# Two blocks on one core: other order at the opening, router, first gather and out-projection, and another form of the last norm

## The chip, the cores and the metric

The kernel runs on one core of a Trainium2 chip. The metric is device time in microseconds (us), lower is better. The engines are named as in the profile: PE multiplies matrices, PEld loads the weights it multiplies by, DVE, ACT and POOL compute elementwise, and SP only issues transfers. ACTq and SPq are the queues on which ACT and SP issue their DMAs; an engine that issues a DMA does nothing else meanwhile. Products are accumulated in PSUM, in eight banks of 128 x 512 floats.

## The reference

512 tokens of width 1024 pass two different blocks. All is fp32.

```python
# first block
h = layer_norm(x, ln_in_g, ln_in_b)
mix = token_mixer(h, ...)              # projections, causal conv, gated delta rule, gating, out-projection
h = layer_norm(ALPHA * h + mix, ...)
ffn = hier_moe(h, ...)                 # router (4 groups x 8), top 2 of 32 experts
h = layer_norm(ALPHA * h + ffn, ln2_g, ln2_b)
# second block, on 16 meta tokens + 512 tokens
xn = rmsnorm(h, norm1_g)
q, k, v, xr, gr, g_merge = split(xn @ w_in)
a = softmax(rope(q) @ rope(k).T) @ v
xc = centred_dwconv(xr, conv_w, conv_b)
r = rg_lru(xc, ..., lam, forward) and (..., reverse)     # uses log_sigmoid(lam)
h = h + merge(a, r, gr, g_merge) @ w_out
h = h + ffn(rmsnorm(h, norm2_g))       # rmsnorm: y = x * rsqrt(mean(x*x) + eps) * g
```

## The kernel before, in words

Every product is made exact to fp32 by splitting both operands into a high part (rounded to fp32r, a form that PE multiplies fast) and a low part (the rest), and by three matmuls per product: low x high, high x high, high x low. The high part of a weight or activation is mostly made by ACT or DVE (a copy), the low part by DVE or POOL (a subtraction of high from raw). Names: `W` raw weights, `WHU`/`WL` high and low of a piece of `w_in`, `HT` turned activations, `HTH`/`HTL` their parts.

Each engine runs a program written out by hand (`s_...` on ACT, `v_...` on DVE, `g_...` on POOL, `p_...` on PE, `q_...` on SP), and engines wait for each other by semaphores. The weights come through a ring of 2 MB slots on SP's queue, load `n` by `q_weight(n)`; `w_room` adds waits to some of them.

The program passes these stages:

- **Opening.** `x` is normed, turned by PE (eight tiles T0 to T7) and split, and the first pieces d0, d1, d2 of `w_in` are split. ACT issues seven loads on its own queue (`L499`, `L500`, `L823` to `L826`) before its first split. POOL also casts a table of constants `lv` (`L517`, used only by the delta rule).
- **Delta rule, merge, first out-projection, norm.**
- **Router.** PE makes the logits tile by tile; DVE adds, finds groups and top 2, ranks tokens and writes the token list `toki`. DVE's cast `oneb` stands ahead of the first logits' evacuation (`L253 ST<-ps,ST`). POOL clears the table `BG[0:64, 8:16]`, from which the gathered rows of expert inputs are read in full (64 rows, two buffers per ring entry).
- **First gather.** POOL gathers 64 rows (0.26 MB) of `h1d` per expert by indirect DMA, each landing in a ring of four. ACT's queue, after PE's last logits, loads rows of `ln2_g`, `ln2_b`, the meta tokens and the rope table; SP's queue loads the weights for slot 6 (2 MB, tile `HT`) at the same time.
- **32 experts**, loop over `b` with PE, DVE and ACT in lockstep, weights streaming.
- **Combine, norm, second block's projections and rope.** `s_lambda` and `v_lambda` make log_sigmoid(lam) for the RG-LRU; they stand at the start of `s_middle`, `v_middle`.
- **Attention**, woven on PE with the convolved columns of `xr` and further projections. `scores(i)` makes the scores of 128 queries into a pair of banks; ACT and DVE make the softmax; `turned(i)` turns the probabilities (form `cst,M`). `pairs` is the list of free pairs of banks. The projection of an x granule of `xr` (kind `"x"`) also takes a pair, which comes free when DVE has read it for the convolution (`L256`, then `L259` x3).
- **RG-LRU**, then **second out-projection**: eight tiles `("out", m, y)`, one per bank, each summed over eight inputs (`VL`, `WO` parts of the merged rows; `WOH`, `WL` parts of `w_out`). The last RG-LRU products (`s6`, `s7`) lie in banks 1 and 0.
- **Last norm**: H is added up by DVE (`v_added`), squared by ACT (`s_squared`), scaled by the inverse rms by ACT (`s_normed3`), turned by PE (`p_turn3`), multiplied by the gain and moved out of PSUM by DVE (`v_gain3`, into `HT`), split high by ACT (`s_turn3`, `XH`) and low by DVE (`v_low3`, `XL`). **FFN** follows, its weight parts in `WS`.

Of the kernel before, what the change touches and what calls it, by code (L numbers as in the profile page):

```python
# [167 lines left out]
def build(nc, a, cst_d, rope_d, out):  # L168
    ctx = ExitStack()
    with ctx:  # L170
# [291 lines left out]
        def q_load():  # L462
            for i in range(NT):
                q.e.dma_start(H[:, i, :], a["x"][0, i * P:(i + 1) * P, :]).then_inc(c_x[i], 16)
                if i == 0:
                    q.e.dma_start(cst[:, :], cst_d[:, 0:C_LV]).then_inc(c_cst, 16)
            for n in range(2):
                q_weight(n)

        def q_zero(part):  # L470

            q.wait_ge(first_done, 2)
# [19 lines left out]
        def s_load():  # L492
# [81 lines left out]
        JOBS = [("d", 0)] + [("T", k) for k in range(8)] + [("d", 1), ("d", 2), "ab"] + [("d", n) for n in range(3, 24)]  # L574
# [108 lines left out]
        def s_evac(n):  # L683
            t, x = B["d", n], xps[n % 3]
            s.wait_ge(*t.full())
            if n < 3:
                s.wait_ge(first_done, 2)
            else:
                s.wait_ge(conv_done, n - 2)
# [415 lines left out]
        def v_head(h):  # L1105
# [6 lines left out]
            v.wait_ge(first_done, 1)  # L1112
# [112 lines left out]
        def g_head(h):  # L1225
# [15 lines left out]
            for n in range(1, 7):  # L1241
                if n == 1:
                    g.wait_ge(first_done, 1)
# [452 lines left out]
        rt_in, rt_out, ms_done, dst_done = sem("router_in"), sem("router_exp"), sem("counts"), sem("rows")  # L1696
# [58 lines left out]
        def s_router():  # L1755
            s.wait_ge(rt_in, 1)
# [4 lines left out]
        def g_router():  # L1761
# [3 lines left out]
            g.e.memset(BG[0:BLK, 8:16, :], 0.0).then_inc(g.up())  # L1765
# [96 lines left out]
        def v_rows():  # L1862
# [6 lines left out]
            v.wait_ge(rt_out, 1)  # L1869
            v.e.tensor_reduce(pgs, gx, AX.X, ADD).then_inc(v.up())  # L1870
            v.wait_ge(rt_out, 2)
# [183 lines left out]
        def s_experts():  # L2055
            s.wait_ge(*B["lg", 3].full())
# [4 lines left out]
            s_expert_x(0)  # L2061
            for b in range(NE):
# [31 lines left out]
        def v_experts():  # L2094
            for b in range(NE):
# [5 lines left out]
                if b == 1:  # L2101
                    v_over_rows()
                if b == NE - 2:
# [18 lines left out]
        def g_experts():  # L2122
# [3 lines left out]
            g.wait_ge(*g.now)  # L2126
# [353 lines left out]
        class Front:  # L2480


            def __init__(self):
# [3 lines left out]
                self.due = []  # L2487

# [138 lines left out]
        def p_second(f, singles, pairs):  # L2627
            for j, (kind, n) in GRAN3:
                o = gr_buf(j)
                p.wait_ge(*gr_low(j))  # L2630
                if kind == "x":
# [9 lines left out]
                    pairs.append(b)  # L2641
                    gr_read[j] = t.full()
# [506 lines left out]
        def v_middle():  # L3149
            f = Front()  # L3150
            ts(v, qg, pcol(QNG), 128.0 ** -0.5, None, MUL, None).then_inc(qg_done)
            v_lambda()
# [8 lines left out]
        def s_middle():  # L3161
            f = Front()
            s_lambda()
# [23 lines left out]
        n2_rms, n2_inv, n2_done = sem("n2_rms"), sem("n2_inverse"), sem("n2_normed")  # L3187
        x3_hi, x3_lo = sem("x3_high"), sem("x3_low")
# [48 lines left out]
        def v_rms3(m):  # L3237
            v.wait_ge(n2_rms, m + 1)
            v.e.reciprocal(ssr[:, m:m + 1], ssr[:, m:m + 1]).then_inc(n2_inv)

        def v_out():
# [6 lines left out]
            v_gain3(0)  # L3248
            v_added(3)
            v_rms3(2)  # L3250
            v_low3(0)
            v_gain3(1)
            v_rms3(3)
            v_low3(1)
            v_gain3(2)
            v_gain3(3)
            v_low3(2)
            v_low3(3)
# [4 lines left out]
        def v_gain3(i):  # L3263
            for h in range(2):
                t = B["x3", i, h]
                v.wait_ge(*t.full())
                tt(v, x3_at(HT, i, h), four(t.at),
                   pc[:, N2G + 4 * h:N2G + 4 * h + 4].unsqueeze(2).to_broadcast([P, 4, P]), MUL).then_inc(t.drained)

        def v_low3(i):  # L3270
            z = slice(i * P, (i + 1) * P)
            v.wait_ge(x3_hi, 2 * i + 2)
            tt(v, XL[:, :, z], HT[:, 0:8, z], XH[:, :, z].bitcast(F32), SUB).then_inc(x3_lo)
# [8 lines left out]
        def s_out():  # L3282
# [5 lines left out]
            s_normed3(0)  # L3288
            s_squared(2)
            s_normed3(1)  # L3290
            s_turn3(0)
            s_squared(3)
            s_normed3(2)
            s_normed3(3)
            s_turn3(1)
            s_turn3(2)
            s_turn3(3)

        def s_normed3(m):
            s.wait_ge(n2_inv, m + 1)  # L3300
            act(XN[:, m, :], H[:, m, :], ACT.Copy, scale=ssr[:, m:m + 1]).then_inc(n2_done)

        def s_turn3(i):
# [283 lines left out]
```

## Time and profile before

| | us |
|---|---|
| median of 3 runs | 2288.48 (2287.21 to 2293.30) |
| profiled execution | 2291.81 |
| its span in the trace | 2290.0 |

| stretch of the span, us | PE busy | DVE busy | PEclk | GB/s |
|---|---|---|---|---|
| 0 to 31.5, opening | 5.89 | 13.91 | 0.83 | 284 |
| 834 to 860.3, router and first gather | 6.77 | 22.49 | 0.50 | 377 |
| 860.3 to 1369, experts | 429.79 | 63.43 | 0.91 | 387 |
| 1530 to 1727, attention | 169.24 | 102.68 | 0.97 | 54 |
| 1860.4 to 1919.7, out-projection and last norm | 50.82 | 38.59 | 0.90 | 87 |
| 1919.7 to 2290, FFN | 363.89 | 111.56 | 0.99 | 83 |

PE is busy for 2064.2 of 2290.0 us (90%). PEclk is the clock that PE was granted, as a share of the full one. In the table a row with PE busy for nearly all of its length is at PE's rate; one where PE is idle has another limit, which the timeline names in brackets.

### The profile page before, as it was taken

The numbers are of one execution on the slowest core, as the hardware profiler recorded it, in microseconds if no ns is written. First come the engines' busy times: TensorE is split into PE (matmuls) and PEld (weight loads), VectorE is DVE, ScalarE is ACT, GpSimd is POOL, SyncE is SP. The second block draws the span as 40 slices with busy tenths as digits, with TensorE's granted clock in tenths as the row PEclk, the third lists the DMA queues.
The fourth block names the chain that finished last, engine by engine and source line by source line (L and its number), as shares of the span: only waits on it lengthen the run. The fifth ranks groups of instructions, "written<-read, shape, count | busy, mean of one in ns | idle before, by whom it ended". The sixth has DMA issues, their size and how long they took to land.

```text
span 2290.0 us, 24322 instructions
## 1 busy us (share of the span) xinstructions
PE 2064.2 (90%) x10160; PEld 1515.5 (66%) x10160; DVE 950.8 (42%) x1370; ACT 644.4 (28%) x969; POOL 454.5 (20%) x311
## 2 busy tenths in 40 slices
PE   5999999999999969888788879898898888999999
PEld 4879888888887753333333337676665666888787
DVE  6864444433323661111011125864554883222333
ACT  3442332321323201000000024343135754222221
POOL 4432132232332511111111011320002310000021
PEclk8899999999999979999899989999999998999999
DMA  4662231221324367999999964302111033322220
GB/s 156 202 184 61 56 88 42 38 74 38 74 37 150 138 246 306 407 410 410 403 412 412 417 280 173 108 2 82 46 47 46 37 111 110 110 94 90 84 82 37
DMA packets 97513, 360.75 MB, mean 158 GB/s; under 512 B 9834, under 2 KB 34572, under 8 KB 85112
## 3 DMA queue, kind: packets, MB, share of 16 engines
q1 hardware_dynamic: 84752, 332.76, 40.4%
q0 software_dynamic: 8240, 19.00, 2.5%
q10 hardware_dynamic: 4408, 7.40, 1.0%
q8 instruction: 82, 1.34, 0.2%
q14 instruction: 31, 0.25, 0.0%
HBM read 338.41 MB, written 29.10 MB: 160 GB/s over the span
## 4 chain that ended last, share of the span: by engine, by line
PE 79%; DVE 9%; ACT 5%; issue 5%; POOL 1%; DMA 1%; ACTq 0%; SPq 0%; DVEq 0%; POOLq 0%
PE ps L269 75%; PE ps L273 4%; ACT ST L265 1%; DVE H L259 1%; ACT L265 1%; DVE ST L253 1%; DVE BG L253 1%; ACT M L265 1%; DVE WL L253 0%; POOL WL L253 0%; DVE ST L2829 0%; DMA BG<-h1d,toki 0%; DVE BG L259 0%; DVE ML L253 0%; ACT M L266 0%
## 5 line engine op out<-in xcount | busy, mean ns | idle before, releaser
L269 PE MATMUL ps<-W,BG 128*64 128x512 f32 x672 | 202.1, 643 | 31.5 <-issue 31.4
L269 PE MATMUL ps<-XH,WS 128*128 128x512 f32 x704 | 218.6, 392 | 0.0
L269 PE MATMUL ps<-HTH,WL 128*128 128x512 f32 x448 | 182.4, 407 | 0.0
L269 PEld LDWEIGHTS ps<-ST 128*128 128x128 f32 x1376 | 168.4, 193 | 8.7 <-POOL ST L253 1.7
L269 PE MATMUL ps<-ST 128*128 128x64 f32 (+1 forms) x1376 | 168.7, 274 | 1.2 <-POOL ST L253 1.0
L269 PEld LDWEIGHTS ps<-XH,WS 128*128 128x128 f32 x704 | 133.5, 190 | 28.0
L269 PE MATMUL ps<-M,BG 128*64 128x512 f32 (+1 forms) x336 | 122.1, 550 | 31.2 <-DVE H L259 13.7
L2100 DVE COPY BG<-ps 128x512 f32<-128x512 f32 x32 | 22.1, 692 | 302.0 <-PE ps L269 302.0
L269 PE MATMUL ps<-XL,WS 128*128 128x512 f32 x352 | 138.3, 393 | 5.0 <-DVE XL L253 5.0
L269 PEld LDWEIGHTS ps<-W,BG 128*64 128x64 f32 x672 | 61.6, 147 | 120.8 <-issue 119.5
L263 ACT ACTIVATE BG<-ps 128x512 f32<-128x512 f32 x48 | 28.5, 595 | 381.3 <-PE ps L273 350.0
L269 PE MATMUL ps<-X2H,GV 128*128 128x512 f32 (+1 forms) x512 | 129.6, 344 | 0.0
L269 PE MATMUL ps<-ST,BG 128*64 128x512 f32 (+2 forms) x304 | 106.1, 566 | 11.7 <-issue 10.9
L269 PE MATMUL ps<-WS,HH 128*128 128x512 f32 x352 | 109.7, 393 | 2.6 <-issue 2.6
L269 PEld LDWEIGHTS ps<-HTH,WL 128*128 128x128 f32 x448 | 88.5, 198 | 20.5
L253 POOL TENSOR_TENSOR WS<-W,WS 128x1024 fp32r<-128x1024 f32 x11 | 26.3, 2392 | 379.8 <-ACT WS L263 379.8
L263 ACT ACTIVATE ST<-ps 128x256 f32<-128x256 f32 (+3 forms) x128 | 44.3, 353 | 196.0 <-PE ps L269 117.2
L269 PEld LDWEIGHTS ps<-X2H,GV 128*128 128x128 f32 x512 | 89.5, 192 | 13.5 <-issue 2.4
L269 PE MATMUL ps<-X2L,GV 128*128 128x512 f32 (+1 forms) x256 | 95.1, 372 | 3.5 <-ACT ST L263 1.8
L273 PEld LDWEIGHTS ps<-cst,BG 64*128 64x128 f32 (+1 forms) x448 | 55.8, 195 | 61.9 <-issue 50.5
L269 PE MATMUL ps<-HT,BG 128*64 128x512 f32 x208 | 86.9, 642 | 9.7 <-issue 9.7
L269 PEld LDWEIGHTS ps<-M,BG 128*64 128x64 f32 (+1 forms) x336 | 48.8, 165 | 67.9 <-issue 39.8
(384 smaller groups left out, 4392.9 us busy)
## 6 DMA issues: line engine op xcount, KB each, us to landing
W<-in_w SPq DMA_DIRECT2D x42, 2048.0 KB, 26.6
W<-in_w_in SPq DMA_DIRECT2D x27, 2048.0 KB, 10.4
ST<-in_w SPq DMA_DIRECT2D x14, 2048.0 KB, 25.6
U<-in_w SPq DMA_DIRECT2D x14, 2048.0 KB, 27.2
M<-in_w SPq DMA_DIRECT2D x13, 2048.0 KB
HT<-in_w SPq DMA_DIRECT2D x13, 2048.0 KB, 27.6
W<-in_w_ffn_in SPq DMA_DIRECT2D x22, 1024.0 KB, 7.7
ypad<-BG SPq DMA_DIRECT2D x23, 512.0 KB, 15.0
```

What stands on the lines that cost most here:

```text
L253: return E.e.tensor_tensor(o, x, y, op)
L259: return v.e.scalar_tensor_tensor(out=o, in0=x, scalar=c, in1=y, op0=op0, op1=op1)
L263: return s.e.activation(o, x, f, scale=scale)
L265: return s.e.activation(o, x, f, bias=bias, scale=scale)
L269: return p.e.matmul(o, lhsT=l, rhs=r, start=start, stop=stop, skip_group_check=True)
L273: return p.e.transpose(o, x, ident[0:n, 0:n])
L2100: v.e.tensor_copy(hs[j], t.at).then_inc(t.drained)
```

## The change

**Opening.** ACT's seven loads go to SP's queue: the weights `W0` first, then the small ones, then `W1`, then the constants `lvf`. ACT splits T0 and T1 first and then weight piece d0; d1 follows T5. PE's and the splitters' common order of jobs (`JOBS`) says the same. POOL's cast `lv` moves to the qk stage (`n == 4`), and `first_done` counts the two events in the other order.

**Router.** The clearing of `BG[0:64, 8:16]` (64 partitions x 4096) becomes an ACT copy of constants times zero, at the head of `s_router`. It counts on `rt_out`, whose later thresholds rise by one.

**First gather.** ACT splits the input of expert 0 (`s_expert_x(0)`) first and then issues its four loads; the weights of slot 6 also wait for the first gather (`c_xg[0]`).

**lambda.** `s_lambda` and `v_lambda` move from the start of the middle to expert 4.

**Attention.** `scores(i)` takes the second free pair where the first is the one that the last x granule used (`f.wide`), and `first` is false there, so that the turn of the tile before comes ahead of the scores.

**Second out-projection.** Tile `("out", m, y)` takes bank 2m+1-y for 2m+y: the first tile takes bank 1.

**Last norm.** SP broadcasts a row of `norm2_g` into free space of `HT`. DVE scales and multiplies by the gain in one pass (`v_rms3`), for ACT's pass and DVE's passes from PSUM; each turned tile has a bank of its own, is split high by ACT from PSUM, and low by DVE from PSUM.

```diff
 q_load:
-            for n in range(2):
-                q_weight(n)
+            q_weight(0)
+            q.e.dma_start(wab_raw, w_in[:, 6144:6272].rearrange("(k p) n -> p k n", p=P)).then_inc(c_ab, 16)
+            q.e.dma_start(abr[:, 0:16], b_in[6144:6160].partition_broadcast(P)).then_inc(c_ab, 16)
...
+            for r, x in enumerate((a["ln_in_g"], a["ln_in_b"])):
+                q.e.dma_start(rows_in0[:, r, :], x.partition_broadcast(P)).then_inc(c_row[r], 16)
+            q_weight(1)
+            q.e.dma_start(lvf, cst_d[:, C_LV:C_N]).then_inc(c_lv, 16)
 ACT, opening:
             for i in range(NT):
                 s_ln(0, i)
-            for r, x in enumerate((a["ln_in_g"], a["ln_in_b"])):
-                s.e.dma_start(rows_in0[:, r, :], x.partition_broadcast(P)).then_inc(c_row[r], 16)
-            s.e.dma_start(lvf, cst_d[:, C_LV:C_N]).then_inc(c_lv, 16)
-            s_ab_load()
-            s_split_w(0)
...
                 s_split(("T", k))
-            s_split_w(1)
+                if k in (1, 5):
+                    s_split_w(k // 4)
 g_load:
-            g.wait_ge(c_lv, 16)
-            g.e.tensor_copy(lv[:, :], lvf).then_inc(first_done)
+            low_split_w(g, 0)
             g.wait_ge(*g.now)
             g.e.memset(xpz, 0.0).then_inc(first_done)
-            low_split_w(g, 0)
             low_split_w(g, 1)
...
-        JOBS = [("d", 0)] + [("T", k) for k in range(8)] + [("d", 1), ("d", 2), "ab"] + ...
+        JOBS = [("T", 0), ("T", 1), ("d", 0)] + [("T", k) for k in range(2, 6)] + [("d", 1), ("T", 6), ("T", 7), ("d", 2), "ab"] + ...
 router:
+            act(BG[0:BLK, 8:16, :], cst[0:BLK, 0:512].unsqueeze(1).to_broadcast([BLK, 8, 512]), ACT.Copy, scale=0.0).then_inc(rt_out)
...
-            g.e.memset(BG[0:BLK, 8:16, :], 0.0).then_inc(g.up())
 s_experts:
-            s.wait_ge(*B["lg", 3].full())
+            s_expert_x(0)
             s_row(0, a["ln2_g"][0])
             s_row(1, a["ln2_b"][0])
             s.e.dma_start(xm, a["meta_tokens_2"]).then_inc(c_m, 16)
             s.e.dma_start(ST[:, 16:18, :].rearrange("p a b -> p (a b)"), rope_d).then_inc(c_rp, 16)
-            s_expert_x(0)
...
+                if b == 4:
+                    s_lambda()
 g_experts:
-            g.wait_ge(*g.now)
+            g.wait_ge(rt_out, 1)
 p_attn:
-                b = pairs.pop(0)
+                b = pairs.pop(1 if pairs[0] == f.wide and len(pairs) > 1 else 0)
...
-                first = i < NT and bool(pairs)
+                first = i < NT and bool(pairs) and pairs[0] != f.wide
 p_out:
-            out2 = [[B.tile(("out", m, y), 2 * m + y) for y in range(2)] for m in range(NT)]
+            out2 = [[B.tile(("out", m, y), 2 * m + 1 - y) for y in range(2)] for m in range(NT)]
 p_turn3:
-                t = B.tile(("x3", i, h), (2 * i + h) % 4)
+                t = B.tile(("x3", i, h), 2 * i + h, nr=2)
 v_rms3:
-            v.e.reciprocal(ssr[:, m:m + 1], ssr[:, m:m + 1]).then_inc(n2_inv)
+            v.e.reciprocal(ssr[:, m:m + 1], ssr[:, m:m + 1]).then_inc(v.up())
+            v.wait_ge(*v.now)
+            v.wait_ge(c_row[1], 80)
+            stt(XN[:, m, :], H[:, m, :], ssr[:, m:m + 1], n2_row, MUL, MUL).then_inc(n2_done)
...
-        def v_gain3(i):
...
+        def v_low3(i, h):
+            t = B["x3", i, h]
+            v.wait_ge(*t.free(1))
+            tt(v, x3_at(XL, i, h), four(t.at), x3_at(XH, i, h).bitcast(F32), SUB).then_inc(t.drained)
...
+        def s_turn3(i, h):
+            s.wait_ge(*B["out", NT - 1 if h else 0, 1 if h else 0].full())
+            t = B["x3", i, h]
+            s.wait_ge(*t.full())
+            act(x3_at(XH, i, h), four(t.at), ACT.Copy).then_inc(t.drained)
 SP:
-            w_room[N_EXP + EXP_SLOTS.index(6)] = [B["lg", i].full() for i in range(NT)]
+            w_room[N_EXP + EXP_SLOTS.index(6)] = [B["lg", i].full() for i in range(NT)] + [(c_xg[0], 16)]
...
+            q.wait_ge(*B["s", 7].full())
+            q.e.dma_start(n2_row, a["norm2_g_2"][0].partition_broadcast(P)).then_inc(c_row[1], 16)
```

What the change moves is shown by each engine's row of instructions. On ACT in the opening, before (`WHU` is the high part of the first weight piece, `HTH` that of turned tiles):

```order
L265 ACTIVATE sm<-sm,cst 128x1 x4
L499 DMA BG<-in_ln_in_g 128x1024
L499 DMA BG<-in_ln_in_b 128x1024
L500 DMA ST<-in_cst 128x896
L823 DMA ST<-in_w_in 128x8x128
L824 DMA ST<-in_b_in 128x16
L825 DMA ST<-in_dn_dt_bias 128x8
L826 DMA ST<-in_dn_a_log 128x8
L263 ACTIVATE WHU<-W 128x1024
L265 ACTIVATE HT<-ps,pc 128x512
L263 ACTIVATE HTH<-HT 128x512 x2
L265 ACTIVATE HT<-ps,pc 128x512
L263 ACTIVATE HTH<-HT 128x512 x2
```

and now:

```order
L265 ACTIVATE sm<-sm,cst 128x1 x4
L265 ACTIVATE HT<-ps,pc 128x512
L263 ACTIVATE HTH<-HT 128x512 x2
L263 ACTIVATE WHU<-W 128x1024
L265 ACTIVATE HT<-ps,pc 128x512
L263 ACTIVATE HTH<-HT 128x512 x2
L265 ACTIVATE HT<-ps,pc 128x512
L263 ACTIVATE HTH<-HT 128x512 x2
L263 ACTIVATE WHU<-W 128x1024
```

The seven DMA rows have gone, and two turned tiles' high parts stand ahead of the first weight piece.

On PE in the attention, at one of 14 places (`M,BG` scores, `cst,M` turn, `X2L,GV` a projection):

```order
 L269 MATMUL ps<-X2L,GV 128x264
 L269 MATMUL ps<-X2H,GV 128x264 x2
-L269 MATMUL ps<-M,BG 128x264 x2
 L273 MATMUL ps<-cst,M 16x128
 L273 MATMUL ps<-cst,M 128x128 x4
+L269 MATMUL ps<-M,BG 128x264 x2
 L269 MATMUL ps<-X2L,GV 128x264
 L269 MATMUL ps<-X2H,GV 128x264 x2
```

The turn of the tile before has moved ahead of the scores.

On DVE in the last norm, before (`H<-H,ps` adds a tile, `HT<-ps,pc` multiplies by the gain, `XL<-HT,XH` makes low parts):

```order
L253 TENSOR_TENSOR H<-H,ps 128x512 x4
L3239 RECIPROCAL sm<-sm 128x1
L253 TENSOR_TENSOR H<-H,ps 128x512 x2
L3239 RECIPROCAL sm<-sm 128x1
L253 TENSOR_TENSOR HT<-ps,pc 128x4x128 x2
L253 TENSOR_TENSOR H<-H,ps 128x512 x2
L3239 RECIPROCAL sm<-sm 128x1
L253 TENSOR_TENSOR XL<-HT,XH 128x8x128
L253 TENSOR_TENSOR HT<-ps,pc 128x4x128 x2
L3239 RECIPROCAL sm<-sm 128x1
L253 TENSOR_TENSOR XL<-HT,XH 128x8x128
L253 TENSOR_TENSOR HT<-ps,pc 128x4x128 x4
```

and now (`M<-H,sm,HT` scales and multiplies by the gain):

```order
L253 TENSOR_TENSOR H<-H,ps 128x512 x4
L3242 RECIPROCAL sm<-sm 128x1
L259 SCALAR_TENSOR_TENSOR M<-H,sm,HT 128x1024
L253 TENSOR_TENSOR H<-H,ps 128x512 x2
L3242 RECIPROCAL sm<-sm 128x1
L259 SCALAR_TENSOR_TENSOR M<-H,sm,HT 128x1024
L3242 RECIPROCAL sm<-sm 128x1
L259 SCALAR_TENSOR_TENSOR M<-H,sm,HT 128x1024
L253 TENSOR_TENSOR H<-H,ps 128x512 x2
L253 TENSOR_TENSOR XL<-ps,XH 128x4x128 x2
L3242 RECIPROCAL sm<-sm 128x1
L259 SCALAR_TENSOR_TENSOR M<-H,sm,HT 128x1024
```

The passes with the gain from PSUM have gone, a scaling pass stands behind each reciprocal, and the low parts are read from PSUM, half a tile at a time.

## Rows read from the trace of the kernel before

**Rows 1.** Page: shares of the chain of waits; GB/s by fortieth of the span.
```profile
PE 79%; DVE 9%; ACT 5%; issue 5%; POOL 1%; DMA 1%; ACTq 0%; SPq 0%; DVEq 0%; POOLq 0%
...
GB/s 156 202 184 61 56 88 42 38 74 38 74 37 150 138 246 306 407 410 410 403 412 412 417 280 173 108 2 82 46 47 46 37 111 110 110 94 90 84 82 37
```

**Rows 2.** Timeline of the opening (start, length, engine, line, operation, [idle <-releaser]).
```profile
16.68 0.81 DVE L256 TENSOR_SCALAR HT<-ps,pc 128x512 f32<-128x512 f32 x1 [0.26 <-PE ps L273]
18.07 6.30 ACTq L824 DMA_DIRECT2D ST<-in_b_in  x1
25.53 1.06 ACT L263 ACTIVATE WHU<-W 128x1024 fp32r<-128x1024 f32 x1 [10.93 <-issue]
27.95 4.05 DVE L253 TENSOR_TENSOR HTL<-HT,HTH 128x512 fp32r<-128x512 f32 x2 [10.46 <-ACT HTH L263]
28.80 2.65 POOL L253 TENSOR_TENSOR WL<-W,WHU 128x1024 fp32r<-128x1024 f32 x1
31.50 0.79 PE L269 MATMUL ps<-HTL,WHU 128*128 128x512 f32 x1 [13.96 <-POOL WL L253]
41.05 0.51 PE L269 MATMUL ps<-HTL,WHU 128*128 128x512 f32 x1 [1.68 <-POOL WL L253]
```

**Rows 3.** Windows: us, busy PE, PEld, DVE, ACT, POOL, then PEclk.
```profile
40.00:75.00 35.00, 33.95 (x143) 27.93 (x144) 33.34 (x27) 14.78 (x20) 22.51 (x11) 0.95 0.27 76
1860.00:1870.00 10.00, 9.62 (x35) 7.85 (x36) 9.86 (x14) 5.43 (x11) 1.51 (x1) 0.79 0.35 115
```

**Rows 4.** Timeline of the router.
```profile
834.35 4.09 DVE L1828 CAST oneb<-cst 128x128 bf16<-128x128 f32 x1
834.82 3.53 POOL L1765 MEMSET BG<- 64x4096 f32 x1
836.80 3.60 PE L269 MATMUL ps<-ST,HT 128*128 128x36 f32 x16 [0.78 <-ACT HT L263]
842.97 0.19 DVE L253 TENSOR_TENSOR ST<-ps,ST 128x36 f32<-128x36 f32 x1
```

**Rows 5.** Timeline and tile view of the first gather.
```profile
840.50 0.33 SPq L367 DMA_DIRECT2D HT<-in_w  x1
851.12 1.01 POOL L2117 DMA_INDIRECT BG<-h1d,toki  x1 [12.76 <-issue]
860.29 1.15 PE L273 MATMUL ps<-cst,BG 64*128 64x64 f32 x8 [10.75 <-DMA BG<-h1d,toki]
...
DMA to landing us min/median/max: 6.9/8.5/10.7
```

**Rows 6.** Timeline of the second rope stage.
```profile
1432.30 0.50 PE L269 MATMUL ps<-X2L,GV 128*128 128x512 f32 x1 [1.33 <-DVE GV L253]
```

**Rows 7.** Page group of attention products, then timeline around one such product.
```profile
L269 PE MATMUL ps<-M,BG 128*64 128x512 f32 (+1 forms) x336 | 122.1, 550 | 31.2 <-DVE H L259 13.7
...
1583.73 2.37 DVE L259 SCALAR_TENSOR_TENSOR H<-ps,pc,H 128x526 f32<-128x526 f32 x3
1586.02 0.15 DVE L2930 RECIPROCAL sm<-sm 128x1 f32<-128x1 f32 x1
1586.15 1.16 PE L269 MATMUL ps<-M,BG 128*128 128x264 f32 x4 [3.33 <-DVE H L259]
1587.89 0.27 ACT L263 ACTIVATE ST<-ps 16x128 f32<-16x128 f32 x1 [7.28 <-PE ps L273]
```

**Rows 8.** Timeline at the start of the second out-projection.
```profile
1852.62 0.60 ACT L265 ACTIVATE ST<-ps 128x512 f32<-128x512 f32 x1
1860.38 0.77 PE L269 MATMUL ps<-WL,VL 128*128 128x512 f32 x1 [8.11 <-ACT ST L265]
```

**Rows 9.** Timeline of the last norm.
```profile
1908.84 1.04 ACT L266 ACTIVATE M<-H 128x1024 f32<-128x1024 f32 x1
1911.39 3.27 PE L273 MATMUL ps<-cst,M 128*128 128x128 f32 x16 [2.77 <-ACT M L263]
1919.70 0.77 PE L269 MATMUL ps<-XL,WS 128*128 128x512 f32 x1 [5.04 <-DVE XL L253]
```

More of the change, by code:

```diff
@@ L569, in v_load @@
             low_split(v, ("T", 7))
-        JOBS = [("d", 0)] + [("T", k) for k in range(8)] + [("d", 1), ("d", 2), "ab"] + [("d", n) for n in range(3, 24)]
+        JOBS = [("T", 0), ("T", 1), ("d", 0)] + [("T", k) for k in range(2, 6)] + [("d", 1), ("T", 6), ("T", 7), ("d", 2), "ab"] + [("d", n) for n in range(3, 24)]
         JOBS += [("v", 0, i) for i in range(4)] + [("v", 1, i) for i in range(4)]
@@ L938, in g_qk @@
                     low_split(g, "ab")
+                if n == 4:
+                    g.wait_ge(c_lv, 16)
+                    g.e.tensor_copy(lv[:, :], lvf).then_inc(first_done)
                 if n in (1, 3, 5, 7):
@@ L1695, in build @@
         c_h1 = sem("h1_stored")
-        rt_in, rt_out, ms_done, dst_done = sem("router_in"), sem("router_exp"), sem("counts"), sem("rows")
+        rt_in, rt_out, ms_done, dst_done = sem("router_in"), sem("router_zero_and_exp"), sem("counts"), sem("rows")
         yrow_done = sem("y_rows")
@@ L2102, in v_experts @@
                     v_over_rows()
+                if b == 4:
+                    v_lambda()
                 if b == NE - 2:
@@ L2487, in __init__ @@
                 self.due = []
+                self.wide = None
         GRAN = [("v", 0), ("k", 0), ("k", 1)] + [("q", n) for n in range(8)] + [("a", n) for n in range(8)] + \
@@ L2641, in p_second @@
                     pairs.append(b)
+                    f.wide = b
                     gr_read[j] = t.full()
@@ L3186, in build @@
         XL = alias("XL", "ST", 10 * 512, [P, 8, T])
[L3187 to L3188 removed]
+        n2_rms, n2_done = sem("n2_rms"), sem("n2_normed")
+        n2_row = HT.rearrange("p a b -> p (a b)")[:, 0:D]
         def p_out():
[L3192 removed]
+            out2 = [[B.tile(("out", m, y), 2 * m + 1 - y) for y in range(2)] for m in range(NT)]
             def add(m, y, k):
@@ L3247, in v_out, with x3_parts @@
             v_rms3(1)
-            v_gain3(0)
+            v_rms3(2)
             v_added(3)
-            v_rms3(2)
-            v_low3(0)
-            v_gain3(1)
+            v_low3(0, 0)
+            v_low3(1, 0)
             v_rms3(3)
[L3254 to L3258, printed above, removed]
+            v_low3(0, 1)
+            v_low3(1, 1)
+            for i in (2, 3):
+                for h in range(2):
+                    v_low3(i, h)
         def x3_at(X, i, h):
             return X[:, 4 * h:4 * h + 4, i * P:(i + 1) * P]
-        def v_gain3(i):
[L3264 to L3273, printed above, removed]
+        def v_low3(i, h):
+            t = B["x3", i, h]
+            v.wait_ge(*t.free(1))
+            tt(v, x3_at(XL, i, h), four(t.at), x3_at(XH, i, h).bitcast(F32), SUB).then_inc(t.drained)
+        def x3_parts(E):
+            for i in range(NT):
+                for h in range(2):
+                    E.wait_ge(*B["x3", i, h].free())
         def s_squared(m):
@@ L3287, in s_out @@
             s_squared(1)
-            s_normed3(0)
             s_squared(2)
-            s_normed3(1)
-            s_turn3(0)
+            s_turn3(0, 0)
+            s_turn3(1, 0)
+            s_turn3(0, 1)
+            s_turn3(1, 1)
             s_squared(3)
[L3293 to L3303, printed above, removed]
-            s.wait_ge(*B["out", NT - 1, 1].full())
-            for h in range(2):
-                s.wait_ge(*B["x3", i, h].free())
-                act(x3_at(XH, i, h), x3_at(HT, i, h), ACT.Copy).then_inc(x3_hi)
+            for i in (2, 3):
+                for h in range(2):
+                    s_turn3(i, h)
+        def s_turn3(i, h):
[3 more added lines that the diff above has]
+            act(x3_at(XH, i, h), four(t.at), ACT.Copy).then_inc(t.drained)
         NF = 22
@@ L3329, in s_split_in @@
             elif n == 2:
-                s.wait_ge(x3_lo, 4)
+                x3_parts(s)
             elif n > 2:
```

24 lines of the change are left out of this document (9 added, 15 removed).

## The prediction

> **What bounds the kernel now.** First the page's shares of the chain: PE has 79% of it, and by the table of stretches its clock is nearly full where it is busy, so matmuls that stay as they are cost what they cost. What a reordering can take is PE's idle time and the low clock behind it. So I read the timeline wherever PE waits at a place that the diff touches, and in each row the idle time in brackets and who ended it. Four such waits carry this forecast: 13.96 us at the first product [rows 2], 10.75 us for the first gather [rows 5], 8.11 us at the second out-projection [rows 8], and 2.77 and 5.04 us in the last norm [rows 9]. GB/s by fortieth shows slices 17 to 23 (span 916 to 1317 us) at 403 to 417 [rows 1]: the experts are the one stage that the weights, not PE, may set.
>
> **Opening: -11.5.** ACT issues its seven loads before any split; one alone holds it 6.30 us, and its first split starts at 25.53 after 10.93 us of idle [rows 2]. But the first turned tile is done at 16.68 + 0.81 = 17.5. Now ACT splits T0 (about half of a 1.06 us pass over 1024, 0.55) to 18.1, T1 to 18.7, the weight piece (1.06) to 19.8; POOL's low part (2.65) ends at 22.5, and PE starts there instead of at 31.50: -9.0. Next, the wait of 1.68 at 41.05 for POOL's second low part goes, since that split now stands earlier; and the low clock after it: the window 40 to 75 has a mean clock of 0.95 [rows 3], which is 0.05 x 35 = 1.75 us lost. PE may now wait about 1.1 for T6 and T7, so 1.68 + 1.75 - 1.1 = 2.3, taken as 2.5 with the rounding of the first. Bounds: -9 if the second wait only moves, -12.5 if T6 and T7 are never late. The loads that SP now issues between the first and the second 2 MB of weights hold SP and not ACT; the second 2 MB serve the fifth piece, tens of us later. The rows of `ln_in` and `lv` are used after the first pieces. All of this is hidden.
>
> DVE's two low parts at 27.95 took 4.05 us while POOL worked 2.65 [rows 2]: take POOL's time off and 0.70 is left for each. DVE stood still while POOL worked, and the same pair meets in the new order. The Trainium skill, "SBUF — State Buffer", section "Who interferes with whom", has it that a DVE operation with two SBUF inputs and a POOL operation that reads SBUF share one pair of ports, and that whoever comes second is blocked fully. The trace agrees (2.65 us). By that rule a DVE low part that starts just ahead of POOL's at 19.8 would put POOL off by up to 0.7, and the sum would be -27.5 instead of -28.2.
>
> **Router: -2.5.** DVE's cast `oneb` takes 4.09 us, to 838.44, beside POOL's clearing (834.82, 3.53 us), and DVE takes the last logits only at 842.97, while PE was done at 836.80 + 3.60 = 840.40 [rows 4]. Without POOL's clearing the cast is short, and DVE is bound by PE: 842.97 - 840.40 = 2.6, taken as 2.5. Bounds: 0 (DVE's own work since 838.4 is what was late) to -2.6. ACT's clearing is 4096 elements wide. At 1.06 for 1024 [rows 2] I estimate up to 4.2 us, from 836.7 (its last split of the turned input, just ahead of PE's row) to 840.9. ACT's next work is the Exp at about 849, so it is hidden by 8 us. If it were late, it would hold the gathers too.
>
> **First gather: -5.** The gather is issued at 851.12 and PE goes on at 860.29: 9.17 us, of which landing is most [rows 5]. In its company are slot 6's weights (2 MB, issued at 840.50) and ACT's row loads. Now the weights wait until the gather has landed, and ACT issues its loads behind the first expert's split. The shortest landing of all 32 gathers is 6.9 us: bound -2.2. All but the 1.01 of issue would be -8.1. In between: 2.1 MB at the 410 GB/s of the expert slices take 5.1 us, which the gather no longer waits for. I take -5, between the nearest row and the far bound, since every landing in the row happened beside streaming weights. The 2 MB are asked for 20 us later; they are for a later expert's slot in the ring.
>
> The Trainium skill, "DMA: Bandwidth & Descriptors", section "Anatomy of one DMA — SWDGE (gpsimd) path", fits such a DMA at 2.0 us plus bytes / 436e3. For 0.26 MB that is an estimate of 2.6 us; this part would be -6.5 and the time 2258.8. No row here shows one so short.
>
> **Lambda: -1.3.** In the rope stage PE waits 1.33 us for DVE's `GV` [rows 6], which stands behind some 5 us of small lambda operations. They go to expert 4, where DVE is idle (63.43 of 508.7 us busy in the experts), so they cost nothing there. Bounds: 0 (DVE's next long reciprocal is late instead) to -4.
>
> **Attention: +4.3.** Before, scores come ahead of the turn and wait for DVE to finish the convolution's reads: 1586.15, [3.33 <-DVE H L259]. There are five such waits, four of them 13.7 us together in the page's group [rows 7], and one more of 3.3. The swap does not remove them. The turn now in front needs the softmax's division, and DVE does that right behind the convolution (reciprocal at 1586.02, scaling 0.5 behind it), in the order it had before. So PE waits to 1586.7 instead of 1586.15, and then the scores wait for ACT's copy of 16 rows (0.27). DVE's work on these scores starts later by the turn's 0.7. Price: +0.5 at each of three such places, +1.2 at a fourth, where the clock is low, -1.8 at one where the convolution's end is not what was late, +0.6 at each of the four turns in the unpaired stretch after them, and +1.7 over the five swaps in the last head, where scores and turns alternate with nothing between. That gives 1.5 + 1.2 - 1.8 + 2.4 + 1.7 = 5.0; some of it runs beside the projections, so I take 4.3. Bounds: 0 to +8 (14 swaps at 0.6).
>
> **Second out-projection: -8.7.** PE waits 8.11 us, from 1852.27 to 1860.38, for ACT's sigmoid of bank 0 (s7). The sigmoid of bank 1 starts at 1852.62 and takes 0.60 [rows 8], so PE could start at 1853.35: -7.0. After the long idle PE's clock is low: 0.79 in the window 1860 to 1870 [rows 3], which is 0.21 x 10 = 2.1 lost. About 1.1 us of wait stays, so I take 1.7 of it. The merged inputs and parts of `w_out` come from ACT and DVE in the same stretch and have been ready one by one since about 1856; if one is late, up to 3 of the 8.7 turn into a wait on `WL` or `VL`. Bank 0's tile is now the second, whose turn is 8 products x 8 inputs later.
>
> **Last norm: -3.5.** Before: PE is done at 1911.39 - 2.77 = 1908.62, starts the FFN at 1919.70: 11.1. Now: ACT has the two first half tiles to split (0.55 each, from 1907.8) and squares the last tile (1.04 [rows 9], 0.5 for sum and root) until 1910.4; DVE's reciprocal 0.15 and the scaling with gain, which I price by the convolution's pass, 2.37 / 3 for 526 [rows 7], so 1.54 for 1024, until 1912.2; PE's turn of the last tile, half of 3.27 [rows 9], until 1913.9; high and low parts of its halves with what is queued in front, 2.3, until 1916.2. That is 19.7 - 16.2 = 3.5. Bounds -1 (the DVE queue is longer than I count) to -5. The 0.5 MB row `n2_row` is asked for near 1852, 48 us ahead of its use.
>
> **Sum.** -11.5 - 2.5 - 5 - 1.3 + 4.3 - 8.7 - 3.5 = -28.2. The profiled execution took 2291.81 (span 2290.0), so it would be 2263.6. It is 3.3 above the median of 2288.48; the median becomes 2260.3. I say 2260.
>
> **Rivals.**
> *The experts swallow what comes before them.* Slices at 410 GB/s [rows 1] speak for a stage whose end the weights fix. Then the 19.0 us of opening, router and gather would be lost, if the weight stream's times stayed. Against: the stream starts when PE frees slots, so it moves with PE. Time 2288.5 - 9.2 = 2279. Chance 0.08.
> *The attention's waits do vanish.* If DVE's division were early and PE filled the wait with the turn, 13.7 + 3.3 = 17.0 would go and the +4.3 too: 2288.5 - 32.5 - 17.0 = 2239. Against: reciprocal at 1586.02, behind the convolution's pass [rows 7]. Chance 0.07.
> *Slower: each swap costs a whole stall.* If the later scores hold DVE, DVE the next convolution and that the next x granule, a swap costs one full wait of 3.32; 14 of them are 46.5. Against the 32.5 of all other parts this gives +14.0: 2302. It decides from 32.5 / 14 = 2.3 us for a swap. For it: PE and DVE do wait for each other in turn there. Against: DVE is busy for half of that stretch (102.68 of 197). Chance 0.03.
> *The forecast* has 0.82.
>
> **Range.** The unknown terms add to about 10 either way when taken together and not all at their ends: 2250 to 2270 is the forecast's own range. To leave out no more than 2 in 10, it goes to 2246 on the side of the vanishing waits and to 2272 on that of the experts. Under 0.3% (7 us) is about what a measurement of this kernel can't tell from no change: 2281.6 to 2295.4. Only the slower rival is beyond, and the experts' rival reaches into it a little: faster 0.96, same 0.01, slower 0.03.
>
> **What would show it.** Opening: PE's first product near 22.5, none of ACT's DMA issues before it; wrong if the wait is for DVE's or POOL's low part at over 24. Router: the cast under 1 us. Gather: landing of the first near 4; if it stays at 7 or more, the company was not the cause. Experts: the distance from first expert to last unchanged. Attention: the waits of 3.3 have moved from `M,BG <- DVE H` to `cst,M <- DVE M L256`, and none is gone. Out-projection: PE begins 7 us earlier against the RG-LRU's end, at a full clock; wrong if a wait of over 2 us for `WL` or `VL` follows. Last norm: 7.6 us from the end of the tile turns to the FFN's first product. The forecast as a whole is wrong if the experts' stretch gets longer by what came before them.

## The result and the profile after

| | before | changed |
|---|---|---|
| median, us | 2290.89 (4 runs, 2287.21 to 2296.97) | 2257.94 (4 runs, 2255.51 to 2263.32) |
| ratio of times | | 0.9857, 95% interval 0.9827 to 0.9886 |
| profiled execution, us (span) | 2291.81 (2290.0) | 2263.32 (2261.5) |

The forecast was 2260 (2263.6 for the profiled execution). The profiled executions differ by 28.5 us. To find where, I took the same PE instruction in both traces and noted how much earlier it starts in the changed kernel. The offset in the table is the start in the changed kernel less the start in the kernel before, and what is gained between two such places belongs to the stage between them. PE's clock phases move these offsets up and down by 1 to 3 us, and in the experts and in the attention's tail by up to 5, as the experiments' traces show where their instructions are the same.

| stage | start of an instruction, before -> changed | offset | gain of the stage | forecast |
|---|---|---|---|---|
| opening | 784.65 -> 772.19 | -12.5 | -12.5 | -11.5 |
| router | 846.09 -> 830.97 | -15.1 | -2.7 | -2.5 |
| first gather | 860.29 -> 839.04 | -21.3 | -6.1 | -5 |
| experts, combine | 1372.91 -> 1353.41 | -19.5 | +1.8 | 0 |
| lambda | 1432.30 -> 1411.51 | -20.8 | -1.3 | -1.3 |
| attention, with convolutions | 1669.21 -> 1636.02 | -33.2 | -12.4 | see below |
| attention, tail | 1727.42 -> 1711.54 | -15.9 | +17.3 | +4.3 for both |
| second out-projection | 1864.28 -> 1840.20 | -24.1 | -8.2 | -8.7 |
| last norm | 1903.88 -> 1878.96, 1919.70 -> 1891.51 | -28.2 | -4.1 | -3.5 |

The opening, on the changed kernel's timeline (start, length, engine, line, operation, [idle <- releaser]); it answers to [rows 2]:

```profile
18.41 1.15 ACT L263 ACTIVATE HTH<-HT 128x512 fp32r<-128x512 f32 x2
19.47 1.04 ACT L263 ACTIVATE WHU<-W 128x1024 fp32r<-128x1024 f32 x1
20.59 2.34 POOL L253 TENSOR_TENSOR WL<-W,WHU 128x1024 fp32r<-128x1024 f32 x1 [13.64 <-ACT WHU L263]
22.99 0.76 PE L269 MATMUL ps<-HTL,WHU 128*128 128x512 f32 x1 [3.36 <-POOL WL L253]
29.51 0.50 PE L269 MATMUL ps<-HTL,WHU 128*128 128x512 f32 x1 [0.57 <-DVE HTL L253]
```
No DMA issue stands before ACT's first splits; PE starts at 22.99 instead of 31.50, and the wait for the second piece, 1.68 before, is 0.57. One more wait went with the diff. Before, ACT's high part was done at 25.53 + 1.06 = 26.59, but POOL began the low part only at 28.80, since it waited until 27.77 for the constants of `lv` and cast them first:

```profile
27.77 0.93 POOL L517 CAST lv<-ST 128x896 bf16<-128x896 f32 x1 [20.82 <-DMA ST<-in_cst]
```
Now POOL begins 0.1 us behind ACT (20.59 after 20.51). The windows of the same matmuls (columns as in [rows 3]) show a full clock in the opening and at the out-projection, and a low one in the attention's tail:

```profile
30.00:65.00 35.00, 35.00 (x162) 28.81 (x160) 32.46 (x29) 15.11 (x21) 22.95 (x12) 1.00 0.39 124
1838.00:1848.00 10.00, 9.96 (x44) 8.27 (x45) 9.83 (x14) 9.96 (x17) 2.97 (x2) 1.00 1.00 347
1684.00:1712.00 28.00, 16.19 (x47) 10.06 (x48) 10.52 (x22) 5.55 (x16) 0.88 (x1) 0.52 0.07 19
```
Router and first gather; they answer to [rows 4, 5]:

```profile
821.89 0.22 DVE L1827 CAST oneb<-cst 128x128 bf16<-128x128 f32 x1
...
823.95 3.60 ACT L263 ACTIVATE BG<-cst 64x4096 f32<-64x4096 f32 x1
827.84 0.20 DVE L253 TENSOR_TENSOR ST<-ps,ST 128x36 f32<-128x36 f32 x1 [1.03 <-PE ps L269]
836.00 1.00 POOL L2119 DMA_INDIRECT BG<-h1d,toki  x1 [13.63 <-issue]
839.04 1.14 PE L273 MATMUL ps<-cst,BG 64*128 64x64 f32 x8 [4.63 <-DMA BG<-h1d,toki]
839.08 0.33 SPq L367 DMA_DIRECT2D HT<-in_w  x1
```
The cast `oneb` takes 0.22 us instead of 4.09. ACT's clearing takes 3.60 and ends before ACT has anything else to do. The gather's data are there 3.04 us after its start instead of 9.17, and the weights of slot 6 are asked for right behind it.

The attention beside a convolution, answering to [rows 7], and then in its tail:

```profile
1559.77 0.71 PE L273 MATMUL ps<-cst,M 128*16 128x128 f32 x5
1560.83 1.16 PE L269 MATMUL ps<-M,BG 128*128 128x264 f32 x4 [0.35 <-ACT ST L263]
1560.83 2.37 DVE L259 SCALAR_TENSOR_TENSOR H<-ps,pc,H 128x526 f32<-128x526 f32 x3
...
1563.34 0.36 PE L269 MATMUL ps<-X2L,GV 128*128 128x264 f32 x1 [1.36 <-DVE H L259]
...
1621.92 1.23 PE L273 MATMUL ps<-cst,M 128*16 128x128 f32 x5 [2.92 <-DVE M L256]
...
1690.80 1.23 PE L273 MATMUL ps<-cst,M 128*16 128x128 f32 x5 [2.09 <-DVE M L256]
1692.38 2.12 PE L269 MATMUL ps<-M,BG 128*128 128x264 f32 x4 [0.36 <-ACT ST L263]
1694.54 0.71 DVE L2930 TENSOR_REDUCE sm<-ps 128x1 f32<-128x528 f32 x1 [3.29 <-PE ps L269]
1695.16 0.68 DVE L2944 COPY ST<-ps 128x512 f32<-128x512 f32 x1
1695.90 1.23 PE L273 MATMUL ps<-cst,M 128*16 128x128 f32 x5 [1.40 <-DVE ST L2944]
```
At 1560.83 the scores start together with the convolution's passes instead of behind them; of 3.33 us only 1.36 are left, in front of the next projection. So it is at three of the five places. At the fourth a turn waits 2.92 us for the division behind the convolution (1621.92), where the scores waited 3.75 before, and nothing is gained: the offset is -29.1 ahead of it and -28.7 behind it. Behind the fifth it is -31.6 (the table's -33.2 stands in the middle of it).

In the tail a turn now waits for something that stands on DVE behind the maximum of the scores made just before it: scores at 1692.38, maximum at 1694.54, then the copy of the turn before out of PSUM at 1695.16, and only then the next turn at 1695.90. At every other turn the releaser is not that copy but a division (`M L256`, 2.09 us of wait at 1690.80). Two tiles took 4.3 us before (1715.45 to 1719.76) and take 10.9 here (1690.80 to 1701.71).

Second out-projection and last norm, answering to [rows 8, 9]:

```profile
1837.29 0.60 ACT L265 ACTIVATE ST<-ps 128x512 f32<-128x512 f32 x1
1838.04 0.47 PE L269 MATMUL ps<-WL,VL 128*128 128x512 f32 x1 [1.09 <-ACT ST L265]
...
1886.38 1.28 DVE L259 SCALAR_TENSOR_TENSOR M<-H,sm,HT 128x1024 f32<-128x1024 f32 x1
1887.72 1.97 PE L273 MATMUL ps<-cst,M 128*128 128x128 f32 x8 [3.23 <-DVE M L259]
1891.51 0.76 PE L269 MATMUL ps<-XL,WS 128*128 128x512 f32 x1 [1.82 <-DVE XL L253]
```
The wait of 8.11 is 1.09; the two waits of 2.77 and 5.04 with 3.27 of turns between (11.1 us) are 3.23 and 1.82 with 1.97 (7.0), since the turn of the third tile now comes ahead of the wait.

### The profile page after: what moved, and what is told of

Read it like the earlier page. It is cut to its first block, busy times and chain, and to the rows that moved or that the text cites. A ratio compares the mean times of both kernels' runs of the same rounds, so it can differ in the third digit from the quotient of the medians.

```text
span 2261.5 us, 24322 instructions
## 1 busy us (share of the span) xinstructions
PE 2066.9 (91%) x10160; PEld 1516.4 (67%) x10160; DVE 943.3 (42%) x1370; ACT 643.6 (28%) x966; POOL 451.9 (20%) x310
## 4 chain that ended last, share of the span: by engine, by line
PE 81%; DVE 8%; issue 5%; ACT 4%; POOL 1%; DMA 0%; PEld 0%; PEldq 0%; SPq 0%; ACTq 0%; DVEq 0%; POOLq 0%
PE ps L269 77%; PE ps L273 4%; ACT ST L265 1%; DVE H L259 1%; ACT L265 1%; DVE ST L253 1%; DVE BG L253 1%; ACT M L265 1%; DVE sm L2930 0%; DVE WL L253 0%; DVE ML L253 0%; POOL WL L253 0%; ACT M L266 0%; DVE H L256 0%; DVE BG L259 0%
## 5 line engine op out<-in xcount | busy, mean ns | idle before, releaser
L263 ACT ACTIVATE BG<-ps 128x512 f32<-128x512 f32 x48 | 28.5, 595 | 377.8 <-PE ps L273 344.2
## 6 DMA issues: line engine op xcount, KB each, us to landing
W<-in_w_in SPq DMA_DIRECT2D x27, 2048.0 KB, 10.3
ypad<-BG SPq DMA_DIRECT2D x23, 512.0 KB, 15.1
```

Source lines behind the costliest of these rows:

```text
L263: return s.e.activation(o, x, f, scale=scale)
```

## The experiments

Each experiment is a kernel that differs from the changed one by the edit shown. Where a kernel was run once, its trace against that of the changed kernel counts, by the offset at the place in question, and not its time, since single times of one kernel differ by up to 10 us here. From here on an offset is the start of an instruction in the experiment less its start in the changed kernel, and places are named by the changed kernel's time.

**The attention.** The rise of 17.3 us in the tail stands where no convolution is left. `f.wide` is never cleared, so it still names a pair of banks that has long been free. In e1 it is cleared when the last x granule is past:

```diff
                 b = pairs.pop(1 if pairs[0] == f.wide and len(pairs) > 1 else 0)
+                if f.out >= N_GELU:
+                    f.wide = None
```

> Edit: as the changed kernel, but f.wide is cleared once the last x granule has been passed, so that scores come first again in the tail of the attention. Theory A: the swap does two opposite things. While convolutions run it takes 2.1 us off at each wait of 3.3 (offset of the two traces from -22.7 to -33.2 between the 1580th and the 1669th us of the kernel before), and in the tail, where no convolution is left, it puts the softmax of one tile and the scores of the next one behind each other and costs 14.0 us. Then this kernel is 14 to 17 us faster than the changed one (near 2242) and the RG-LRU starts at an offset of about -32. Theory B: the tail's 14 us are a debt, work that the earlier part left over and that must be done somewhere; then the time stays within 4 us of 2258.

In e2 both lines of the attention are those of the kernel before:

```diff
-                b = pairs.pop(1 if pairs[0] == f.wide and len(pairs) > 1 else 0)
+                b = pairs.pop(0)
...
-                first = i < NT and bool(pairs) and pairs[0] != f.wide
+                first = i < NT and bool(pairs)
```

> Edit: the changed kernel with the attention's order of the kernel before (pairs.pop(0), scores always first). Theory A (gain of 12 in the convolutions, loss of 17 after them): 5 us faster than the changed kernel, near 2253, with the five waits of 3.3 us for DVE H L259 / ST L259 back and no wait of 1.4 for ST L2944 in the tail. Theory B (the forecast's reading: each swap costs 0.5 to 1.2, nothing is gained): also about 4 faster, but with the first three waits costing no more PE time than in the changed kernel. The offsets at the single places tell them apart: A wants +2.1 at each of the first three, B -0.5.

> The changed kernel as it is, on the same chip as the two variants: 2258 within 3 us, 1.4% under the kernel before. It is the base for both comparisons.

| kernel (5 runs each, same chip) | median, us | lowest to highest | ratio to before, 95% interval |
|---|---|---|---|
| e3, changed kernel again | 2262.24 | 2256.29 to 2265.96 | 0.9876 (0.9855 to 0.9896) |
| e2, attention as before | 2259.81 | 2256.23 to 2266.28 | 0.9871 (0.9850 to 0.9892) |
| e1, scores first in the tail | 2247.47 | 2243.10 to 2251.60 | 0.9807 (0.9791 to 0.9823) |

e3 is 2262.24 where I expected 2258 within 3, so I compare with e3 and not with the first result. e1 is 14.8 us faster than e3, as theory A wanted, and their ranges don't meet; theory B, a debt that must be paid somewhere, falls. Its trace in the tail:

```profile
1689.51 0.71 PE L273 MATMUL ps<-cst,M 128*16 128x128 f32 x5
1690.57 1.16 PE L269 MATMUL ps<-M,BG 128*128 128x264 f32 x4 [0.35 <-ACT ST L263]
1693.82 0.71 PE L273 MATMUL ps<-cst,M 128*16 128x128 f32 x5
```
Two tiles take 4.3 us again, with no wait but the 0.35 for ACT's copy. e2 is 2.4 us faster than e3, not 5, and its time alone can't tell a gain of 5 from none. Its trace can: beside the convolutions the waits are back, and the offset goes from +4.2 at 1530 to +14.0 at 1636 and to -2.9 at 1712.

```profile
1567.45 1.16 PE L269 MATMUL ps<-M,BG 128*128 128x264 f32 x4 [3.33 <-DVE H L259]
```
So the swap wins about 9 to 12 us beside the convolutions (2.1 at each of the first three waits, +4.5 -2.4 in e2's offsets) and loses up to 17 in the tail.

How much it loses there depends on the clock. e4, e6, e7 and e9 have the changed kernel's attention too, and against the kernel before their tails lose 12.3 to 13.1 us where the changed kernel's loses 17.3 (e3 and e5: 17.3 too). The waits are the same, but two tiles take 7.9 us (8.1 in e7) for 10.9, and most turns 0.71 us for 1.23. In e4:

```profile
1697.79 0.71 PE L273 MATMUL ps<-cst,M 128*16 128x128 f32 x5 [2.08 <-DVE M L256]
```
In the window 1684 to 1712 the mean granted clock is 0.77 in e4 and 0.52 in the changed kernel. So of the 3.3 us that a tile costs more, about 1.8 is the order and 1.5 the low clock.

Is it the order or the other pair of banks that wins? e8 is e1 with one line changed:

```diff
-                b = pairs.pop(1 if pairs[0] == f.wide and len(pairs) > 1 else 0)
+                b = pairs.pop(0)
```

> Edit: as the variant that keeps scores first in the tail (e1), but scores(i) takes the first free pair as in the kernel before; only the order of turn and scores is swapped. Theory A1 (the other pair of banks is what removes the wait: the turn in front gives back a pair that no convolution reads): the scores wait again for DVE's convolution, 2.6 us (3.3 less the turn of 0.7) at each of the first three places, and the gain there is at most 0.7 instead of 2.1 each, 8 to 10 us slower than e1 in all. Theory A2 (the order alone does it, since the turn fills the wait and starts DVE's next operation earlier): within 2 us of e1.

```profile
1558.33 2.37 DVE L259 SCALAR_TENSOR_TENSOR H<-ps,pc,H 128x526 f32<-128x526 f32 x3
1560.75 2.13 PE L269 MATMUL ps<-M,BG 128*128 128x264 f32 x4 [2.78 <-DVE H L259]
...
1575.88 1.16 PE L269 MATMUL ps<-M,BG 128*128 128x264 f32 x4 [2.78 <-DVE H L259]
```
The wait for the convolution is back at 2.78, that is 3.33 less what the turn hides. Against e1's own trace e8 falls back by 10.3 us between the 1559th and the 1642nd us of e1 (from -4.5 to +5.7), as A1 wanted, though a single place costs less than 2.6 net, since the next projection then doesn't wait: +2.4 at the scores, -1.0 to -1.7 right behind. The rest is lost in the projections that follow, at a low clock: 0.57 in e8's window 1562.3 to 1567.5, 1.00 in e1's 1566.3 to 1570. The order is only the means: the turn in front gives back a pair that no convolution reads, and the scores' taking that pair is the gain.

**The first gather.** e4 drops the new wait, e5 puts ACT's loads in front again:

```diff
e4:
-            w_room[N_EXP + EXP_SLOTS.index(6)] = [B["lg", i].full() for i in range(NT)] + [(c_xg[0], 16)]
+            w_room[N_EXP + EXP_SLOTS.index(6)] = [B["lg", i].full() for i in range(NT)]
e5:
-            s_expert_x(0)
+            s.wait_ge(*B["lg", 3].full())
             s_row(0, a["ln2_g"][0])
...
             s.e.dma_start(ST[:, 16:18, :].rearrange("p a b -> p (a b)"), rope_d).then_inc(c_rp, 16)
+            s_expert_x(0)
```

> Edit: the changed kernel without the wait of slot 6's weights for the first gather; ACT's loads still stand behind the first expert's input. Theory A (the 2 MB of weights are the company that made the gather land in 9.2 us instead of 3.0): the gather lands 5 to 6 us later again, the experts start 5 to 6 later, and the whole is up to 6 slower. Theory B (ACT's four loads were the company): the gather still lands in 3 to 4 us and nothing else changes.

> Edit: the changed kernel with ACT's four loads (rows, meta tokens, rope table) ahead of the first expert's input again; slot 6's weights still wait for the gather. Theory A: the gather is hardly touched, at most 1 us. Theory B: it lands 5 to 6 later, since 1.6 MB stand in the queues at the same time.

```profile
832.64 1.00 POOL L2119 DMA_INDIRECT BG<-h1d,toki  x1 [13.66 <-issue]
839.47 1.15 PE L273 MATMUL ps<-cst,BG 64*128 64x64 f32 x8 [8.41 <-DMA BG<-h1d,toki]
```

```profile
832.28 0.33 ACTq L485 DMA_DIRECT2D ST<-in_ln_g  x1
834.23 1.01 POOL L2120 DMA_INDIRECT BG<-h1d,toki  x1 [13.64 <-issue]
842.94 1.15 PE L273 MATMUL ps<-cst,BG 64*128 64x64 f32 x8 [10.30 <-DMA BG<-h1d,toki]
```
From the gather's start to PE's first use of it: 3.04 us in the changed kernel, 6.83 in e4 (weights in company), 8.71 in e5 (ACT's loads in company), 9.17 before (both). The offsets at this use say the same: e4 falls back by 3.8 (from -3.4 to +0.4) and e5 by 5.7 (from -1.8 to +3.9). Neither theory is right as it stood: each company alone gives most of the delay, ACT's loads the larger part, and removing only one would have won at most 2.3 us of the 6.1.

**The router.** e6 gives the clearing back to POOL (the diff's router lines undone).

> Edit: the changed kernel with POOL clearing the 64x4096 table again instead of ACT. Theory A (DVE's cast of oneb stands still while POOL writes, and the last logits wait behind the cast): the cast takes about 4.1 us again and the ranks come 2.5 us later, everything behind shifts by 2.5. Rival: the last logits are late for another reason (DVE's small operations on the first three tiles); then the cast is longer but the ranks move by under 1 us.

```profile
821.00 4.08 DVE L1827 CAST oneb<-cst 128x128 bf16<-128x128 f32 x1
821.47 3.53 POOL L1764 MEMSET BG<- 64x4096 f32 x1
832.71 0.31 PE L269 MATMUL ps<-mfb,sub 128*128 128x160 bf16 x1 [5.93 <-DVE mfb L253]
```
The cast is at 4.08 us again, next to POOL's 3.53, and the offset at the ranks' first product grows by 2.8 (from -1.0 to +1.7): theory A.

**The out-projection.** e7 gives tile (m, y) bank 2m+y again.

> Edit: the changed kernel with tile (m, y) of the second out-projection in bank 2m+y again. Theory A: PE waits for the sigmoid of bank 0 again, about 8.1 us instead of about 1.1, and the clock is low after it: 8.6 us slower, near 2266. Rival: other inputs of the out-projection (mix, low part of w_out) were what came last in the changed kernel, so that the wait is only partly the bank's: under 5 slower.

```profile
1840.38 0.76 PE L269 MATMUL ps<-WL,VL 128*128 128x512 f32 x1 [8.12 <-ACT ST L265]
```
8.12 us of wait; the offset grows by 7.0 at this instruction and 2.0 more in the next 3 us, where the clock is low: 9.0 us from one bank number.

**The opening.** e9 has SP's loads but the old order of splits; e10 has the new order, but all seven loads on ACT's queue in front of its first split.

> Edit: the changed kernel with the loads on SP's queue, but the weight piece d0 split before the turned tiles and d1 after all eight, as in the kernel before. Theory A (ACT's DMA issues were the whole delay of the first product): PE's first product still comes at 22 to 24, and the second piece's wait (1.68 in the kernel before) is back. Theory B (the order of splits mattered for the first product too, since d0's weights land late or hold the tiles' splits): first product over 25.

> Edit: the changed kernel with the seven loads on ACT's queue again, ahead of its first split, in the new order of splits. Theory A: ACT's first split starts after 25 us again and the first product comes near 31.5, so 8.5 us later than in the changed kernel. Rival: the loads wait in the queues of the DMA engines, not on ACT; then moving them back changes little, and the first product comes before 26.

```profile
21.50 0.47 PE L269 MATMUL ps<-HTL,WHU 128*128 128x512 f32 x1 [2.41 <-DVE HTL L253]
31.01 0.50 PE L269 MATMUL ps<-HTL,WHU 128*128 128x512 f32 x1 [1.71 <-POOL WL L253]
```

```profile
17.61 6.01 ACTq L502 DMA_DIRECT2D ST<-in_b_in  x1
30.79 0.79 PE L269 MATMUL ps<-HTL,WHU 128*128 128x512 f32 x1 [13.60 <-POOL WL L253]
```
In e9 the first product is even earlier (21.50; theory A had 22 to 24), but the second piece costs a wait of 1.71, and at 31 both kernels are level. At 83 e9 is 1.7 us behind the changed kernel's trace, but so is e3, the changed kernel again (1.8): with the loads on SP's queue no gain from the order of splits is shown. In e10 one issue holds ACT for 6.01 us and PE starts 7.8 late, and at 83 it is still 7.7 late. So the loads' place is worth about 8 us. At the same instruction e10 is 5.6 ahead of the kernel before, 0.7 of it at the first product. That is the order of splits and the moved cast `lv` together, which e10 both keeps (there POOL starts right behind ACT's high part, at 28.40); no run separates them.

**The last norm.** e11 has all of the changed kernel but the last norm of the kernel before.

> Edit: the changed kernel with the last norm of the kernel before (ACT scales, DVE multiplies by the gain out of PSUM, both parts from HT), everything else as changed. Theory A: from the last product of the out-projection to the first of the FFN it takes 3.3 to 4.5 us more (waits of 2.8 and 5.0 back), as the two traces say. Rival: the gain there came from the other bank order of the out-projection, not from the norm's new form: under 1 us more.

```profile
1883.89 3.51 PE L273 MATMUL ps<-cst,M 128*128 128x128 f32 x16 [2.77 <-ACT M L263]
1892.20 0.77 PE L269 MATMUL ps<-XL,WS 128*128 128x512 f32 x1 [4.80 <-DVE XL L253]
```
The waits are 2.77 and 4.80 again, and the offset grows by 3.3 us between the first turn (1878.96 in the changed kernel) and the FFN's first product: theory A.

## Why the forecast was right, and where it was not

**The time was right, and five of its seven terms.** Opening -12.5 for -11.5 (-12.9 to -15.9 by the other traces with this opening, -8.2 in e2, of which more below). ACT's issues are the cause of most of it (e10), and the second wait and its low clock went (0.95 became 1.00). The -9.0 at the first product holds, since it was worked out from when PE would start now. But it is not all ACT's: 2.2 us of it were POOL's wait for `lv` and its cast, which stood on the same path and which the forecast doesn't name. Router -2.7 for -2.5, by the mechanism named (e6). Lambda -1.3, as the row said; no run takes this part back. Out-projection -8.2 for -8.7, wait and clock both (e7). Last norm -3.3 to -4.1 for -3.5: 7.0 us where 7.6 were worked out, the scaling at 1.28 us where 1.54 was taken from the narrower pass.

**First gather: mechanism right, size small.** Forecast -5, measured -6.1. I held 6.9, the shortest landing in the old trace, against 410 GB/s of company and stayed in the middle. All those landings had company; alone it took 3.04 us to first use. The Trainium skill, "DMA: Bandwidth & Descriptors", section "Anatomy of one DMA — SWDGE (gpsimd) path", gave an estimate of 2.6 us by its fit, and the run shows 3.04 from the start of the issue to first use: here the page was nearer than my bound.

**Attention: the total was near and the reasons were wrong.** Forecast +4.3, measured +4.9 (from -20.8 to -15.9), as the sum of -12.4 and +17.3. The step that failed is "the turn now in front needs the softmax's division, and DVE does that right behind the convolution". The division at 1586.02 [rows 7] is of another tile; the one that the turn needs was done at 1580.98, before the convolution began. This is the row of the kernel before that I passed over:

```profile
1580.49 0.49 DVE L256 TENSOR_SCALAR M<-M,sm 128x528 f32<-128x528 f32 x1
```
So the turn goes at once, and the scores behind it take another pair. Only at the fourth place did the forecast's picture come true (2.92 at 1621.92). In the tail I priced the five swaps at 1.7 in all, though I had written that nothing stands between scores and turns there. e1's trace shows what was lost: with scores first, two tiles are in flight and PE works while DVE divides; with the turn first they are in a row, 3.3 us more for each tile, 1.5 of it by a clock of 0.52 in the window 1684 to 1712. The rival "the waits do vanish" was right in its first half (e2, e8) and the slower one in its picture of a full stall for each swap (3.0 to 3.6 us at each of the last four, e1), but each held in one stretch only. That two errors of about 15 us cancelled is luck. So is how near +4.9 is: in e4, e6, e7 and e9 the same attention comes to between -0.2 and +1.3 by the same count.

**The experts did not swallow anything.** The offset goes in at -21.3 and comes out at -19.5: the stretch took 514.4 us for 512.6. In the other traces with these experts it took 512.1 (e5, which enters it 3.9 late) to 519.3 (e10, 5.0 late), so 2 us is inside this spread. The rival wanted 19. It is dead here.

## What to carry to other kernels

Before you reorder two instructions of one engine, find in the trace which tile each one waits for, not which operation of that kind is nearest; where they alternate, look apart at the stretch with work between them and the one without. A rule that is meant for one stretch needs its end: two lines that clear the mark made this kernel 14.8 us faster again (e1, 2247.47); the opening, its largest part, had brought 12.5 in the profiled execution. And what the first transfer of a stage takes should be judged by what is queued beside it: one gather cost 9.2 us in company and 3.0 alone.

## What the runs showed of the chip beyond that

**Two engines' passes exclude each other, and a race decides which waits.** In e2, which leaves the opening as it is, DVE's two low parts took twice as long as in the changed kernel; this is e2, then the changed kernel:

```profile
26.30 2.42 POOL L253 TENSOR_TENSOR WL<-W,WHU 128x1024 fp32r<-128x1024 f32 x1 [3.52 <-ACT WHU L263]
27.58 4.50 DVE L253 TENSOR_TENSOR HTL<-HT,HTH 128x512 fp32r<-128x512 f32 x2 [0.86 <-ACT HTH L263]
29.16 2.36 POOL L253 TENSOR_TENSOR WL<-W,WHU 128x1024 fp32r<-128x1024 f32 x1 [0.45 <-ACT WHU L263]
32.13 0.50 PE L269 MATMUL ps<-HTL,WHU 128*128 128x512 f32 x1 [1.85 <-DVE HTL L253]
```

```profile
27.79 2.27 DVE L253 TENSOR_TENSOR HTL<-HT,HTH 128x512 fp32r<-128x512 f32 x2 [0.87 <-ACT HTH L263]
29.37 2.95 POOL L253 TENSOR_TENSOR WL<-W,WHU 128x1024 fp32r<-128x1024 f32 x1 [0.47 <-ACT WHU L263]
```
In e2 POOL's third subtraction came ahead of DVE's second low part, DVE's two took 2.2 us longer, PE waited 1.85 more, and with the clock behind it e2 was 4.8 us late at 72 us, counted from where the two traces start. The Trainium skill, "SBUF — State Buffer", section "Who interferes with whom", says that whoever comes second is blocked for the whole instruction. By that rule the length 4.50 is 2 x 0.7 plus what is left of POOL's two passes, 1.1 us until 28.72 and about 2.0 until 31.52, and the trace agrees. Of ten traces with this opening one shows it. The times of one kernel may spread by this, which no run here isolates.

**Company costs a small transfer more than its bytes.** ACT's four loads, with 8.71 us, delayed the gather more than 2 MB of weights, with 6.83 us (e5, e4). Bytes alone would put it the other way round: between the gather's start and PE's use of it the DMA engines moved about 1.9 MB in e5 (219 GB/s) and 2.2 MB in e4 (320 GB/s), and they were busy for 0.81 and 0.88 of the time. So ACT's loads held them longer for each byte. That e4's weights were asked for 8 us ahead of the gather (824.54, 832.64) didn't get them out of its way: the engines still moved 467 GB/s from 834 to 836. Which of ACT's loads is the slow one, no run separates. In the changed kernel the engines were busy for 0.16 of those 3.04 us.
